# Sample state updates from stacked rounded rows, and the new keys' values in four column strips

## The reference

```
p = (p[:, 0] - lam * p[:, 1])
out = einsum('bhqk,bkhe->bqhe', p[..., :past], vp) + einsum('bhqk,bkhe->bqhe', p[..., past:], v_new)
```

```
k_dec = k * exp(log_g[:, None] * (c - 1.0 - idx))
s_new = exp(log_g * c) * s_prev + einsum('bhjd,bhje->bhde', k_dec, v)        # c = 8, sum over the 8 tokens j
```

## Time and profile before

| | |
|---|---|
| median of 3 runs | 3517.52 us (3515.86 to 3519.99) |
| the profiled execution | 3512.0 us |
| its span in the profile | 3510.2 us, 1.8 us less |
| TensorE busy (PE) | 3355.9 us, 96% |
| VectorE busy (DVE) | 2127.8 us, 61% |
| ScalarE busy (ACT) | 1118.8 us, 32% |
| GpSimd busy (POOL) | 200.6 us, 6% |
| mean granted TensorE clock | 0.991 |
| HBM traffic over the span | 192 GB/s |

### The profile page before, as it was taken

The page is one execution under the profiler, slowest core; times in us unless marked ns, Lnnn a source line. Parts: engine busy times, 40 slices in busy tenths (PEclk is TensorE's granted clock), DMA queues, the critical chain, the costliest instruction groups (busy, mean ns, idle before and its releaser), DMA issues.

```text
span 3510.2 us, 65225 instructions
## 1 busy us (share of the span) xinstructions
PE 3355.9 (96%) x25284; PEld 2965.2 (84%) x25284; DVE 2127.8 (61%) x3225; ACT 1118.8 (32%) x1646; POOL 200.6 (6%) x157
## 2 busy tenths in 40 slices
PE   7998999999999999888999999999999999999998
PEld 7987888788778878678999999999999777777787
DVE  4466565656665566437666666767666345666666
ACT  4222222222222232214333333333332343322323
POOL 1000000000000000002000000000000222222200
PEclk9999999999999999999999999999999999999999
DMA  5466888788788888754523333333334565555534
GB/s 179 151 202 208 279 273 273 247 285 269 259 265 286 263 272 268 256 190 144 165 100 124 117 111 111 125 122 118 108 116 167 199 212 204 199 201 196 195 128 156
DMA packets 477798, 679.31 MB, mean 194 GB/s; under 512 B 32561, under 2 KB 283570, under 8 KB 474354
## 3 DMA queue, kind: packets, MB, share of 16 engines
q1 hardware_dynamic: 434882, 618.88, 53.5%
q10 hardware_dynamic: 42192, 55.98, 4.5%
q0 software_dynamic: 416, 0.28, 0.1%
HBM read 583.92 MB, written 89.52 MB: 192 GB/s over the span
## 4 chain that ended last, share of the span: by engine, by line
PE 85%; DVE 6%; issue 3%; DMA 2%; ACT 2%; SPq 1%; POOL 0%; DVEq 0%; ACTq 0%; POOLq 0%
PE low_banks L1270 57%; PE high_banks L1270 26%; PE high_banks L1273 3%; DVE WL L1900 2%; DMA area<-in_cache_v 1%; SPq L1158 1%; DVE area L2001 1%; ACT WH L1583 1%; DMA WR<-in_w_in_ret 0%; DVE x_rows L1927 0%; DVE area L2263 0%; DVE area L1974 0%; DVE area L2336 0%; DMA area<-in_x_prompt 0%; DVE XL L2344 0%
## 5 line engine op out<-in xcount | busy, mean ns | idle before, releaser
L1270 PE MATMUL low_banks<-XH,WH 128*128 128x288 f32 (+2 forms) x4632 | 1125.5, 310 | 38.7 <-DVE WL L1900 12.1
L1270 PE MATMUL low_banks<-XH,WL 128*128 128x288 f32 (+2 forms) x4632 | 1063.3, 297 | 0.0
L1270 PE MATMUL low_banks<-XL,WH 128*128 128x288 f32 (+2 forms) x4632 | 1060.8, 296 | 0.0
L1270 PEld LDWEIGHTS low_banks<-XH,WH 128*128 128x128 f32 x4632 | 769.2, 190 | 186.7 <-issue 153.9
L1270 PEld LDWEIGHTS low_banks<-XH,WL 128*128 128x128 f32 x4632 | 772.4, 190 | 0.0
L1270 PEld LDWEIGHTS low_banks<-XL,WH 128*128 128x128 f32 x4632 | 772.1, 190 | 0.0
L1270 PE MATMUL high_banks<-area 128*32 128x256 f32 (+8 forms) x4720 | 628.9, 466 | 30.8 <-DMA area<-in_cache_v 12.4
L1270 PEld LDWEIGHTS high_banks<-area 128*32 128x32 f32 (+2 forms) x4720 | 272.9, 139 | 246.1 <-issue 178.5
L1583 ACT ACTIVATE WH<-WR 128x1024 fp32r<-128x1024 f32 x272 | 287.4, 1056 | 543.4 <-PE low_banks L1270 451.6
L1900 DVE TENSOR_TENSOR WL<-WR,WH 128x1024 fp32r<-128x1024 f32 x272 | 348.1, 1280 | 133.0 <-ACT WH L1583 127.4
L2001 DVE STREAM_TRANSPOSE area<-area 128x512 f32<-128x512 f32 x512 | 334.5, 690 | 108.3 <-PE high_banks L1270 63.9
(11 more groups left out here) (184 smaller groups left out, 3256.9 us busy)
## 6 DMA issues: line engine op xcount, KB each, us to landing
area<-in_cache_k SPq DMA_DIRECT2D x512, 256.0 KB, 4.9
area<-in_cache_v SPq DMA_DIRECT2D x512, 256.0 KB, 5.3
area<-in_w_in_ret SPq DMA_DIRECT2D x162, 512.0 KB, 5.7
WR<-in_w_in_attn SPq DMA_DIRECT2D x136, 512.0 KB, 5.3
WR<-in_w_out_ret SPq DMA_DIRECT2D x66, 512.0 KB, 3.8
area<-in_state_ret SPq DMA_DIRECT2D x64, 512.0 KB, 7.5
out<-area SPq DMA_DIRECT2D x64, 512.0 KB, 5.5
WR<-in_w_in_ret SPq DMA_DIRECT2D x38, 512.0 KB, 3.7
```

The lines of the kernel that those rows point to most:

```text
L1270: return nc.tensor.matmul(out, a, b, start=start, stop=stop, skip_group_check=True)
```

## The change

Layer 0: the new keys' values become four matmuls of 64 keys x 32 rows x 128 columns, one for each quarter of the columns, the n-th into the n-th strip of partitions, 32 times.

Layer 1: keys and values of the sample tokens are split into a rounded (float32r) and a remaining part, and each band of 32 rows holds three times the 8 rows of one sequence (and 8 rows of zeros): keys rounded, remaining, rounded against values rounded, rounded, remaining. One float32r matmul per pair of bank and half then takes the place of one float32 matmul. For that
- `load_v3` (slot 5, SyncE) loads the values from HBM with 8 DMAs of 32 rows x 512 each; `pad_v` (slot 14): ScalarE copies 128x1024 twice (rounded, and scaled), VectorE joins them in one instruction of 128x1024;
- `store_k` (slot 10) stores the keys to HBM, `load_k3` (slot 13) loads them back, when the store has landed, with 8 DMAs; `pad_k` (slot 21): ScalarE two copies of 128x512, VectorE one instruction of 128x512;
- `pad_rows`, `rs_mask` and two of the four clearings in `pads` go;
- `rs_state` moves one slot back, to 25, 34, 43 and 51. At slots 43 and 51 it thus comes behind the tile of slots 42 and 50 and its `split_w`, and at slot 51 it stands directly ahead of `gate` t=4. `store_state_p` stays at slot 50, now ahead of `rs_state`.

```diff
     put(9, Stage("rs_keys"))
-    put(10, Stage("pad_rows"))
-    put(17, Stage("rs_mask"))
+    put(5, Stage("load_v3"))
+    put(10, Stage("store_k"))
+    put(13, Stage("load_k3"))
+    put(14, Stage("pad_v"))
+    put(21, Stage("pad_k"))
     put(21, Stage("rs_out"))
     put(27, Stage("ret_rstd", t=4, n=1))
     norms = [Stage("ret_norm", t=t) for t in range(5)]
@@ -601,7 +606,7 @@
         put(14 + 9 * c, Stage("ret_scores", c=c))
         put(18 + 9 * c, Stage("ret_out", c=c))
         put(19 + 9 * c, Stage("ret_state", c=c))
-        put(24 + 9 * c - (c == 3), Stage("rs_state", g_=c // 2, e=c % 2))
+        put(25 + 9 * c - (c == 3), Stage("rs_state", g_=c // 2, e=c % 2))
...
-            def pad_rows(g):
+            def thrice(to, rows):
+                per = rows.rearrange("(j g i) n -> j g i n", g=2, i=NQ)
+                for j, n in itertools.product(range(4), range(2)):
+                    yield to[32 * j:32 * j + 32, n, :], per[j, n].rearrange("(o i) n -> o i n", o=1).broadcast_to([4, NQ, rows.shape[1]])
+
+            def load_v3(g):
+                for n in ("full6", "full7", "rvn_in"):
+                    sp.wait_ge(sem[n], c.before(n))
+                for to, rows in thrice(v3, values_d[SEQ:T, 512 * g:512 * g + 512]):
+                    sp.dma_start(to, rows).then_inc(sem["v3_in"], 16)
+
+            def store_k(g):
                 sp.wait_ge(sem["drained5"], c.before("drained5"))
+                sp.wait_ge(sem["k3_in"], c.before("k3_in"))
+                sp.dma_start(keys_d, kn_s[:]).then_inc(sem["k_out"], 16)
+
+            def load_k3(g):
+                sp.wait_ge(sem["k_out"], c.before("k_out"))
                 sp.wait_ge(sem["kz_ready"], c.before("kz_ready"))
-                for n in ("full4", "full5", "full6", "full7", "rvn_in"):
-                    sp.wait_ge(sem[n], c.before(n))
-                for j in range(4):
-                    rows, padded = slice(16 * j, 16 * j + 16), slice(32 * j, 32 * j + 16)
-                    sp.dma_start(knz[padded, :], kn_s[rows, :]).then_inc(sem["padded_in"], 16)
-                    sp.dma_start(rvz[padded, :], rvn[rows, 4, :]).then_inc(sem["padded_in"], 16)
+                for to, rows in thrice(k3, keys_d):
+                    sp.dma_start(to, rows).then_inc(sem["k3_in"], 16)
...
-                              start=i == 0, stop=i == NGROUP - 1 and cc > 0)
+                              start=i == 0, stop=False)
                 if i == NGROUP - 1:
                     pe.wait_ge(sem["drained5"], c.after(turned[4], "drained5"))
-                    last = mm(bank[7][0:32, :], mine(e_new[:]), vS[0:SMP, :], start=False)
+                    for cc in range(4):
+                        cols = slice(128 * cc, 128 * cc + 128)
+                        last = mm(bank[7][32 * cc:32 * cc + 32, cols], mine(e_new[:]), vS[0:SMP, cols], start=False)
...
-                    mm(bank[4 + j][:, :], kz[rows, g_, e * 128:(e + 1) * 128], rvz[rows, :]).then_inc(sem[f"full{4 + j}"], 1)
+                    mm(bank[4 + j][:, :], kz[rows, g_, e * 128:(e + 1) * 128], vz[rows, g_, :]).then_inc(sem[f"full{4 + j}"], 1)
...
+            def pad_v(g):
+                act.wait_ge(sem["v3_in"], c.before("v3_in"))
+                act.wait_ge(sem["head_in"], c.before("head_in"))
+                for n in range(4, 8):
+                    act.wait_ge(sem[f"full{n}"], c.before(f"full{n}"))
+                copy(vz, v3)
+                copy(v3, v3, scale=hc[:, 387:388]).then_inc(sem["pad_hi"], 1)
+
+            def pad_k(g):
+                act.wait_ge(sem["k3_in"], c.before("k3_in"))
+                copy(kz, k3, scale=hc[:, 384:385])
+                copy(k3, k3, scale=hc[:, 385:386]).then_inc(sem["pad_hi"], 1)
...
-            def rs_mask(g):
-                dve.wait_ge(sem["padded_in"], c.before("padded_in"))
-                for n in range(4, 8):
-                    dve.wait_ge(sem[f"full{n}"], c.before(f"full{n}"))
-                for b_ in range(2):
-                    ins = v.tensor_scalar(kz[:, b_, :], knz[:], hc[:, 384 + b_:385 + b_], None, MUL)
-                    if b_:
-                        ins.then_inc(sem["kz_ready"], 1)
-                    else:
-                        o.link(ins)
+            def pad_v(g):
+                dve.wait_ge(sem["pad_hi"], c.done("pad_hi"))
+                v.scalar_tensor_tensor(out=vz, in0=vz.bitcast(f32), scalar=hc[:, 388:389], in1=v3, op0=MUL, op1=ADD).then_inc(sem["kz_ready"], 1)
+
+            def pad_k(g):
+                dve.wait_ge(sem["pad_hi"], c.done("pad_hi"))
+                v.scalar_tensor_tensor(out=kz, in0=kz.bitcast(f32), scalar=hc[:, 386:387], in1=k3, op0=MUL, op1=ADD).then_inc(sem["kz_ready"], 1)
```

More of the change, by code:

```diff
@@ L26 @@
 MASKED = -1e30
-HC = 128 + 128 + 64 + 64 + 2 + 1 + 2
+HC = 128 + 128 + 64 + 64 + 5 + 1 + 2
 KRING, VRING = 4, 8
@@ L76, in shape_tables @@
         r = np.arange(128)
-        kz = np.where((r % 32 < 2 * NQ)[:, None] & ((r % 32 // NQ)[:, None] == np.arange(2)[None]),
-                      np.exp(lg * (NQ - 1.0 - r % NQ))[:, None], 0) * w
+        third = r % 32 // NQ
+        fade = np.where(third < 3, np.exp(lg * (NQ - 1.0 - r % NQ)), 0) * w
+        kz = np.stack([fade, fade * (third == 1), np.array([1.0, -1, 1, 0])[third], third == 2, np.array([1.0, 1, -1, 0])[third]], 1)
         heads.append(np.concatenate([dec, spread(np.exp(lg * (i + 1))), spread(np.exp(lg * (t + 1.0))), pad(decs), pad(kz),
@@ L169, in adds @@
         "rs_keys": {"full4": 1, "full5": 1, "drained4": 1, "drained5": 1, "qd_ready": 1},
-        "pad_rows": {"padded_in": 128}, "rs_mask": {"kz_ready": 1},
+        "load_v3": {"v3_in": 128}, "store_k": {"k_out": 16}, "load_k3": {"k3_in": 128},
+        "pad_v": {"pad_hi": 1, "kz_ready": 1}, "pad_k": {"pad_hi": 1, "kz_ready": 1},
         "ret_scores": {"full4": 1, "full5": 1, "drained4": 1, "drained5": 1},
@@ L866, in hybrid_step_kernel @@
     values_d = nc.dram_tensor("retention_values", (T, 2 * D), f32, kind="Internal").ap()
+    keys_d = nc.dram_tensor("retention_sample_keys", (SMP, 256), f32, kind="Internal").ap()
     x1_d = nc.dram_tensor("x_between_layers", (T, D), f32, kind="Internal").ap()
@@ L986, in hybrid_step_kernel @@
         used[0] = after_inputs
-        rvz = lay("rvz", [128, 512])
+        rounded = mixes.rearrange("p a k n -> p (a k n)")
+        kz, vz = [rounded[:, at:at + 2 * n].rearrange("p (g n) -> p g n", g=2) for at, n in ((kz_at, 256), (vz_at, 512))]
+        v3 = oN[:, 2:4, :]
         rst, decay8 = lay("rst", [128, 10]), lay("decay8_sb", [128, HEADS])
@@ L1100, in hybrid_step_kernel @@
         SP_NAMES = [n for n in sem_names if "_in" in n]
-        ACT_NAMES = [n for n in sem_names if "_out" in n] + ["w_hi", "half_act", "mix_hi", "g_ready", "o_scaled", "exp_ready", "e_rows", "pv_drained", "y_sq", "y_scaled", "x_sq", "x_scaled_act", "x_hi",
+        ACT_NAMES = [n for n in sem_names if "_out" in n] + ["w_hi", "half_act", "pad_hi", "mix_hi", "g_ready", "o_scaled", "exp_ready", "e_rows", "pv_drained", "y_sq", "y_scaled", "x_sq", "x_scaled_act", "x_hi",
                                                             "proj0_drained", "proj1_drained"]
@@ L1207, in load_rvn @@
                 wait_stored(stored)
-                for n in ("w_used", "full4", "full5", "full6", "padded_in"):
+                for n in ("w_used", "full4", "full5", "full6"):
                     sp.wait_ge(sem[n], c.before(n))
@@ L1256, in _ @@
                                   load_x_tile=load_x_tile, load_norm=load_norm, load_pages=load_pages, load_rope=load_rope, load_tables=load_tables,
-                                  load_quads=load_quads, store_state=store_state, load_qk=load_qk, load_rvn=load_rvn, load_g4=load_g4, pad_rows=pad_rows, pads=pads))
+                                  load_quads=load_quads, store_state=store_state, load_qk=load_qk, load_rvn=load_rvn, load_g4=load_g4, load_v3=load_v3, store_k=store_k, load_k3=load_k3, pads=pads))
         @block.tensor
@@ L1774, in rs_keys @@
                 act.wait_ge(sem["full5"], c.done("full5"))
-                act.wait_ge(sem["padded_in"], c.before("padded_in"))
+                act.wait_ge(sem["k_out"], c.before("k_out"))
                 copy(kn_s[:], bank[5][0:SMP, 0:256]).then_inc(sem["drained5"], 1)
+            def pad_v(g):
[9 more added lines that the diff above has]
+                copy(k3, k3, scale=hc[:, 385:386]).then_inc(sem["pad_hi"], 1)
             def ret_scores(g, c_):
                 act.wait_ge(sem["full5"], c.done("full5"))
-                copy(kd[:], bank[5][:, 0:256], scale=hc[:, 386:387]).then_inc(sem["drained5"], 1)
+                copy(kd[:], bank[5][:, 0:256], scale=hc[:, 389:390]).then_inc(sem["drained5"], 1)
             def square(c_):
@@ L1855, in _ @@
                                 ret_scores=lambda g, c: ret_scores(g, c), ret_out=lambda g, c: ret_out(g, c),
-                                rs_keys=rs_keys, rs_out=rs_out, store_state_p=store_state_p, split_g=split_g,
```

(6 more changed lines are left out.)

11 lines of the change are left out of this document (5 added, 6 removed).

## The result

The changed kernel takes 3547.5 us (median of six runs, 3544.6 to 3557.9) beside 3515.2 us (3510.6 to 3520.0) of the kernel before on the same chip: a ratio of 1.0092 [1.0081, 1.0103]. It is about 32 us **slower**; the forecast was 3508, faster by some 10. The two profiled executions differ by 36.0 us (spans 3546.2 and 3510.2). One execution of the kernel of experiment 9 was slow (5449 us) and is left out of its time and ratio; all the others count.

A forecast was written before the change was run, and what follows sets the result against it. TensorE, busy 96% of the span, was taken to bound the kernel. Terms -18.0 - 1.9 + 5.4 - 2.3 + 6.6 + 0.5 = -9.7 us took the 3517.5 us median to 3508, range 3496 to 3520.

The forecast's parts named there:

- part 1: Layer 0 attention: new keys' values in four strips, 0.44 us a set for 1.07, giving -18.0 us (-15 to -22).
- `ret_out`, slots 25, 34, 43: Layer 1 heads: -1.9 us at slots 25 and 34, +5.4 at slot 43, where WL runs ahead of the additions.
- gate, slot 51: Layer 1: gate waits for bank 6 right behind rs_state, WL no longer runs into rope; -2.3 us (-7 to +5).
- clock behind the gates: Layer 1: longer gate waits lower the clock to 1.2 GHz after six of eight; +6.6 us (0 to +14).
- late rows: Layer 1: supply of the stacked key and value rows by DMA and copies, forecast at +0.5 us (0 to +15).
- 4 x 0.55 = 2.2 us are lost: Layer 0: part of the strips' gain not coming through, before transposes waiting for VectorE and beside value loads.
- Part 2: Layer 1: rs_state in one pass; the 0.8 us saved come back as a wait for VectorE's additions.
- 45 said: Layer 1 sign: TensorE's waits for the additions of rs_state rise from 10.7 to some 45 us.
- the upper end that the text named: Slot 51: a WL that meets rope at slot 50 holds the additions back; +0.9 to +1.9 us in the first three heads.
- Part 3: Layer 1: supply of the stacked rows; value rows land near 2977, keys at 2987, needed at 2995; +0.5 us.
- the cover: Layer 1, slot 14: mask of ret_scores done at 2981.2, ret_out wants it at 2981.86; 0.7 us to spare.
- The named rival: Slot 14: stacked rows land late, pad_v holds copy and mask; 3 us later costs 18 us, 3526; chance 0.12.

The follow-up runs named there:

- experiment 9: Kernel before with the new keys' values in four column strips and the gate's first tile at slot 54 in place of 51: 3498.3 us, 0.9957.
- experiment 1: Kernel before with the new keys' values in four column strips and nothing else: 3506.7 us, 0.9970.
- experiment 2: Kernel before with only rs_state one slot later (25, 34, 43, 51), still float32 with four passes: 3543.1 us, 1.0078.
- experiment 3: Changed kernel with rs_state back at slots 24, 33, 42 and 50: 3530.6 us, 1.0042 against the kernel before.
- 6: Changed kernel with the gate's first tile at slot 54 in place of 51: 3533.8 us, 1.0059 against the kernel before.
- experiment 7: Kernel before with the gate's first tile at slot 50 in place of 51, nothing else changed: 3518.0 us, 1.0004.
- 4: Changed kernel with pad_v at slot 20 in place of 14 and pad_k at 22 in place of 21: 3526.0 us, 1.0032 against the kernel before.
- 10: Changed kernel with pad_v at slot 18, rs_state at 24, 33, 42, 50 and the gate's first tile at 54: 3486.4 us, 0.9921 against the kernel before.
- experiment 8: Changed kernel with the four later state loads at slots 8, 10, 12, 14 in place of 4, 7, 10, 13: 3567.3 us, 1.0153.
- experiment 5: Changed kernel with the value rows in their own buffer, loaded at slot 49 of the head before, pad_v at slot 2: 3533.3 us, 1.0051.

## Why the prediction was wrong

| Term, us | forecast | profile | by |
|---|---|---|---|
| part 1 | -18.0 | -12.3 (mean of 11: -11.3) | experiment 1 |
| `ret_out`, slots 25, 34, 43 | -1.9 + 5.4 = +3.5 | 18.5 of waits, 24 x 0.63 saved, -1.4 for the mask (L2238): +2.0 | 2, 3 |
| gate, slot 51 | -2.3 | +12.3 of waits, 8 x 0.63 saved, -4.4 for L1964, -3.1 for L2306: -0.3 | 2, 6, 7 |
| clock behind the gates | +6.6 | (34.0 - 6.8) / 2 = +13.6 | 7 |
| late rows | +0.5 | +22.4 of waits, and 17.0 / 2 = 8.5 of clock: +30.9 | 4, 10 |

With 1.7 us of clock at the last accumulation, and 0.8 us more in a few waits at the end, layer 1 sums to +48.7; the profile has +48.2. Between the forecast of -9.7 and the profile's +36.0 lie 45.7 us; 30.4 of them are the late rows, 7.0 the clock behind the gates, 5.7 part 1.

**Part 1.** The price of a set was right. Wrong was "4 x 0.55 = 2.2 us are lost": 8.5 are. The text looked for waits directly behind the 32 places, and found p_mix; it left out the clock, which is low for 9.3 us more over the whole stretch with strips (mean of 11 against 34.0 in each of the three without; one of the 11 has 34.0 too). Why it falls more often there is not shown.

**Part 2.** The mechanism, "the 0.8 us saved come back as a wait for VectorE's additions", holds in every head, with 2.21 us from the additions' start to the release, and slot 43 with WL ahead as well. The waits for L2295 are 41.5 us (45 said). The pass takes 0.51 us, within its bounds of 0.29 and 1.14. At the gate two sizes were off by a little. The five later heads lose 0.36 us each (2.33 - 1.34 - 0.63) where 0.1 was said. The three first wait 3.6 to 3.8 us, the upper end that the text named: WL at slot 50 runs beside GpSimd's `rope`. VectorE's WL in head 2 ends at 2958.45, 1.08 us behind the GpSimd instruction that ends at 2957.37:
```profile
2955.95 1.42 POOL L2461 TENSOR_TENSOR area<-area 128x576 f32<-128x576 f32 x1
```
By the Trainium skill (SBUF — State Buffer, "SBUF: two separate sides") the two exclude each other for the whole instruction; the trace agrees. The other two counts of this step came true: the accumulations wait 4.4 us less (4.8 said), the other wait in head 0 behind the same WL 3.1 us less (2.4 said).

**The clock.** "I take a fall after six of the eight": all eight gates fell, two of them for 6.8 us, with nothing to subtract but 3.4. The term was mis-sized, 13.6 for 6.6, and the late rows added falls of their own, which the rival's price did not include.

**Part 3 is the step that failed.** It said that `load_v3` "lands with 2 to 3 us more, near 2977 on head 3's scale" and that there are "0.7 us to spare, so the cover holds". The issues came where they were expected: they begin 5 us in front of the `rs_keys` copy (2978.03, 2983.07), which in the kernel before stands at 2974.39, and end 5.2 us later. The landing took a median of 5.5 us behind the last, and in head 3 6.6: the rows were 3 to 4 us late. The named rival is what happened: 2.3 us at 3 us late was its price for a head, 2.8 us the measured mean wait; its chance was 0.12. The 2 to 3 us were taken from the small DMAs between two places of SBUF. These rows come from DRAM, and a nearer line was at hand in the same view of the kernel before (KB of one, median us to landing):
```profile
area<-in_state_ret SPq DMA_DIRECT2D x61, 512.0 KB, 7.6
area<-area SPq DMA_DIRECT2D x32, 32.0 KB, 2.4
area<-retention_values SPq DMA_DIRECT2D x7, 128.0 KB, 8.7
```
The last is the load of 128 KB from the very tensor. With it the rival would have been the forecast. How much of the landing is the DMA's own and how much its neighbours' is open: moving the state load ahead (experiment 8) changed little, but 3.2 us in head 0 of experiment 5 and up to 10.6 us in experiment 3 show that it is not fixed.

## What to carry to other kernels

Before a consumer is put behind a DMA in an engine's queue, take its landing time from a row with the same source and the same surroundings (it moved from 3.2 to 10.6 us here with the kernel around it), and list what else stands behind the consumer: the copy that waits costs nothing, the unrelated copy and mask behind it cost 22 us and a share of the clock. A faster matmul whose result is drained by another engine gained here only where the drain did not start later, so the pass must not be moved later in the order along with it: left at its old slots, with the rows' work behind the mask and the gate behind the drain, the same matmuls turned 32 us of loss into 28 us of gain. And waits stand in a row: remove the earlier ones and a later wait can take back part of it, so measure the remedies together.

## What the runs showed of the hardware

- A wait of 2.3 us at the gate was followed by 3.4 us at the level of 1.2 GHz in five of eight heads (experiment 7); after waits of 2.3 to 3.8 us it was so in eight of eight, twice for 6.8 us (the changed kernel), and in six of eight in experiment 2, after 1.34 us in none of seven before (in head 0 a wait of 3.8 us followed). It is not only the gate: waits of 1.9 to 2.1 us for accumulations had it behind them in three of five heads (experiment 9). Ahead of `ret_out` in the changed kernel waits of 2.73 and 2.84 us had none behind them and one of 2.82 us had, so the length of the wait alone does not decide.
- Eight DMAs of 64 KB from DRAM were ready 4.3 to 7.8 us after the last issue in experiment 8 and the changed kernel, 6.0 to 10.6 us in experiment 3, and once 3.2 us (experiment 5). The Trainium skill (DMA: Bandwidth & Descriptors, "Anatomy of one DMA — SWDGE (gpsimd) path") gives about 2 us plus bytes / 436e3 (in us) for one, measured on GpSimd's path; by it 64 KB would be there in 2.2 us, an estimate. No run here isolates a single DMA; beside others the measured times are mostly two to three and a half times that, so this formula would not have given the landing here.
- Storing 64 KB of keys to DRAM took a median of 7.1 us to land, 8.0 us in head 3; there the load that waits for it held SyncE from 2987.4 to 2992.4, the next weight load behind it.
